# Expert tokens fetched by row numbers, and expert weights loaded in 8 KB runs, in a two-layer decoder trunk

## The chip, the core and the metric

The kernel runs on one core of a Trainium2 chip. It is written by hand, engine by engine: TensorE (PE) multiplies, VectorE (DVE) and ScalarE (ACT) read its results out of the eight PSUM banks, GpSimd (POOL) does small jobs, and SyncE (SP) issues nearly all transfers from memory. Engines wait for each other by semaphores that are written out in the code. The metric is the time of one execution on the device in microseconds.

## What is computed

A sequence of 256 tokens of width 1024, all in float32, goes through two layers. Layer 0 mixes tokens by a gated recurrence and a state-space scan, layer 1 by RWKV-7. Each layer ends in a mixture of experts, which is where most of the time and of the weights are:

```python
def grouped_moe(h, router_w, router_b, w1, w3, w2):      # 16 experts, D=1024, F=512, each token takes 2
    logits = jnp.einsum('bsd,de->bse', h, router_w) + router_b
    probs = jax.nn.softmax(logits, axis=-1)
    ...
    top_w, top_i = lax.top_k(masked, TOP_K)
    ...
    hidden = silu(einsum('bsd,edf->bsef', h, w1)) * einsum('bsd,edf->bsef', h, w3)
    hidden = hidden * gates[..., None]
    return jnp.einsum('bsef,efd->bsd', hidden, w2)
```

## The kernel before

**Experts in blocks.** The 16 experts are taken in 8 pairs. A block is 128 slots: 64 for tokens of the one expert of a pair and 64 for the other. A pair takes one block, or more where an expert has over 64 tokens; with these inputs layer 0 has 9 blocks (the fourth pair has two) and layer 1 has 8. Tables made on the chip give each pair's number of blocks, and every engine loops over the blocks of a layer.

**A block on PE** (`block_of_pair`, L1118). First the products with w1 and with w3, L1141, 16 matmuls each of 128x64 weights by 512 columns (a profile's x32 for each, since a float32 matmul stands as two records). Then `gather` (L1063, L1066): the tokens of the next block are brought into the transposed form `hgT` that the products want, by 16 matmuls of the normed tokens `hN` with a one-hot matrix `pick`. Then `scatter(0)` (L1074), which adds the previous block's result back to its tokens by another one-hot matrix `spread`; 4 transposes of the hidden layer (L1153); `scatter(1)`; and the product with w2 (L1165), first for columns 0 to 511 of the output, then for the rest.

**Around it.** DVE multiplies the two halves of the hidden layer (L2328), copies the second half of the gathered tokens (`take_b`, L2301), makes the next `pick` (`pick_step`, L2293, L2296) and the next `spread` (L2337 to L2341). ACT does the SiLU, copies the first half (`take_a`), the transposed hidden layer and half of the result. POOL has nothing to do in the blocks.

**Weights.** w1, w3 and w2 of an expert are 2 MB each. Ten slots of 2 MB hold them, that is five "doubles" (one matrix of both experts of a pair, two slots). A layer has 24 doubles. The first five are loaded before the blocks start. Double number d (from 5) goes where double d-5 was, when the last block of that pair is through with it: `w1_done`, `w3_done` and `down_half` tell SP (L626 to L631). A double goes out as four transfers of 1 MB. In each, row k*128+p of a matrix goes to partition p (`row_block`), so a transfer is made of runs of 512 numbers, 2 KB.

**Another place that is touched.** In the RWKV-7 layer, PE makes the gate (`gate_second`, four banks), which ACT reads out by `evac_T(ggT, ...)` (L1633), and then starts the next projection (`rkv(1, 0)`, L784) in the same four banks. Between them ACT takes roots of key lengths (`key_root`, L1610 and L1616), of which numbers 2 and 3 wait for DVE (L2406).

## Time and profile before

| | |
|---|---|
| median of 3 runs | 1210.8 us (1210.73 to 1210.84) |
| the profiled execution | 1203.89 us, of which the span from first to last instruction is 1202.2 us |
| granted TensorE clock over the span | 0.972 |
| moved by the transfer engines | 309.56 MB |
| L1141 and L1165, products of the experts | 1088 and 544 matmul records |
| L1066, one-hot gathers | 608 records, 72.7 us |

"Busy" in a row is the time in which an engine has an instruction in it. The chain is the work that ended last, followed back from the last instruction to whatever released it. A time in brackets behind a row is how long the engine sat idle before it, and what ended that. The granted clock is 1.00 at 2.4 GHz and 0.50 at 1.2 GHz.

### The profile page before, as it was taken

What the parts mean: (1) busy time and instruction counts of PE and PEld (TensorE: products, weight loads), DVE (VectorE), ACT (ScalarE), POOL (GpSimd) and SP (SyncE); (2) the same over time, 40 slices, a digit from 0 to 9 for tenths busy, and PEclk for the clock granted to TensorE, in tenths of its full rate; (3) what the DMA queues carried; (4) which work ended last, traced back from release to release, by engine and by line L of the source; (5) the groups of instructions that cost most, each with busy time, mean ns of one, the idle gap of its engine ahead of it and who ended that gap; (6) DMA issues with size and microseconds to landing.
All of it is one profiled execution on the core that took longest, in us unless ns stands there. A gap on an engine that the chain in (4) does not pass through costs nothing.

```text
span 1202.2 us, 15755 instructions
## 1 busy us (share of the span) xinstructions
PE 1144.8 (95%) x6555; PEld 758.4 (63%) x6555; DVE 418.5 (35%) x932; ACT 266.6 (22%) x439; POOL 90.7 (8%) x120
## 2 busy tenths in 40 slices
PE   5899999998989999999999897999989999999997
PEld 3686798984478844444444576848878744444454
DVE  0364853365720321111111485565432411111113
ACT  2222110414220311111111344233230311111112
POOL 5002221200000100000000102111000100000000
PEclk9899999999989899999999998999989899999998
DMA  9797774439967379959999712000069599999991
GB/s 351 264 340 279 280 271 149 141 129 370 402 236 262 119 291 387 386 217 349 389 386 338 286 71 70 1 0 2 7 261 387 186 335 387 387 386 386 386 382 42
DMA packets 157180, 309.56 MB, mean 258 GB/s; under 512 B 9568, under 2 KB 10940, under 8 KB 157116
## 3 DMA queue, kind: packets, MB, share of 16 engines
q1 hardware_dynamic: 156320, 307.39, 70.3%
q8 instruction: 51, 0.84, 0.3%
q10 hardware_dynamic: 796, 1.23, 0.3%
q14 instruction: 13, 0.11, 0.0%
HBM read 307.55 MB, written 1.05 MB: 257 GB/s over the span
## 4 chain that ended last, share of the span: by engine, by line
PE 90%; DVE 3%; SPq 3%; ACT 2%; DMA 1%; issue 1%; ACTq 1%; DVEq 0%
PE bank L1141 19%; PE bank L784 16%; PE bank L1165 10%; PE bank L845 7%; PE bank L1074 7%; PE bank L1066 6%; PE bank L795 5%; PE bank L911 2%; PE bank L817 1%; PE bank L754 1%; PE bank L1427 1%; SPq L509 1%; PE bank L1417 1%; PE bank L1335 1%; DMA ring<-in_ev_w_in 1%
## 5 line engine op out<-in xcount | busy, mean ns | idle before, releaser
L784 PE MATMUL bank<-arena,ring 128*128 128x256 f32 x960 | 216.2, 387 | 10.4 <-ACT arena L1633 6.3
L784 PEld LDWEIGHTS bank<-arena,ring 128*128 128x128 f32 x960 | 185.6, 195 | 37.7 <-issue 9.9
L1141 PE MATMUL bank<-ring,arena 128*64 128x512 f32 x704 | 153.7, 592 | 0.0
L1141 PEld LDWEIGHTS bank<-ring,arena 128*64 128x64 f32 x704 | 50.4, 137 | 99.6 <-issue 99.4
L2328 DVE TENSOR_TENSOR arena<-arena,bank 128x512 f32<-128x512 f32 x17 | 11.7, 687 | 220.7 <-PE bank L1141 220.7
L845 PE MATMUL bank<-arena,ring 128*128 128x256 f32 x384 | 85.4, 386 | 2.9 <-DVE arena L2551 2.9
L1074 PE MATMUL bank<-arena 128*128 128x256 f32 x336 | 84.2, 398 | 1.7 <-issue 1.7
L1141 PE MATMUL bank<-arena 128*64 128x512 f32 x384 | 84.1, 592 | 0.0
L845 PEld LDWEIGHTS bank<-arena,ring 128*128 128x128 f32 x384 | 74.4, 194 | 13.7 <-issue 3.2
L1066 PEld LDWEIGHTS bank<-arena 128*128 128x128 f32 x608 | 69.3, 192 | 13.8 <-issue 13.8
L1066 PE MATMUL bank<-arena 128*128 128x128 f32 x608 | 72.7, 278 | 0.0
L1074 PEld LDWEIGHTS bank<-arena 128*128 128x128 f32 x336 | 64.6, 202 | 11.6 <-issue 3.4
L1165 PE MATMUL bank<-ring,arena 128*64 128x512 f32 x288 | 63.8, 595 | 0.0
L1141 PEld LDWEIGHTS bank<-arena 128*64 128x64 f32 x384 | 27.6, 137 | 54.8 <-issue 54.8
L1165 PE MATMUL bank<-arena 128*64 128x512 f32 x256 | 56.7, 595 | 0.0
L795 PE MATMUL bank<-ring,arena 128*128 128x512 f32 x128 | 55.5, 592 | 0.0
L2344 DVE COPY arena<-bank 128x512 f32<-128x512 f32 x17 | 11.8, 692 | 102.3 <-PE bank L1165 102.3
L1165 PEld LDWEIGHTS bank<-ring,arena 128*64 128x64 f32 x288 | 19.9, 137 | 39.0 <-issue 39.0
L1971 DVE SCALAR_TENSOR_TENSOR arena<-ring,csilu,arena 128x512 f32<-128x512 f32 x56 | 43.6, 779 | 2.0
L1752 ACT ACTIVATE arena<-bank 128x512 f32<-128x512 f32 x19 | 11.3, 597 | 142.5 <-PE bank L1066 142.5
L795 PEld LDWEIGHTS bank<-ring,arena 128*128 128x128 f32 x128 | 24.2, 190 | 29.3 <-issue 29.2
L1762 ACT ACTIVATE arena<-bank 128x512 f32<-128x512 f32 x17 | 10.1, 597 | 139.5 <-PE bank L1141 139.5
(366 smaller groups left out, 1302.7 us busy)
## 6 DMA issues: line engine op xcount, KB each, us to landing
ring<-in_moe_w SPq DMA_DIRECT2D x112, 1024.0 KB, 14.2
arena<-in_moe_w SPq DMA_DIRECT2D x80, 1024.0 KB, 14.3
ring<-in_mod_w SPq DMA_DIRECT2D x24, 2048.0 KB, 11.1
ring<-in_ev_w_in SPq DMA_DIRECT2D x13, 2048.0 KB, 13.1
ring<-in_od_w_rkv SPq DMA_DIRECT2D x6, 2048.0 KB, 13.5
ring<-in_ev_w_out SPq DMA_DIRECT2D x4, 2048.0 KB, 17.3
ring<-in_od_w_o SPq DMA_DIRECT2D x2, 2048.0 KB, 10.5
arena<-in_x ACTq DMA_DIRECT2D x1, 1024.0 KB, 9.1
```

The source lines that it names most:

```text
L509: sp.dma_start(dst, src).then_inc(tile_landed[slot], 16)
L754: mm = pe.matmul(norm_total(k), ones[:, 0:P], squares[:, b, :], start=(b == 0), stop=(b == KB - 1))
L784: mm = pe.matmul(ps[:, c * S:(c + 1) * S], w_cols(slot)[:, k, (2 * half + c) * P:(2 * half + c + 1) * P], src[:, k, :], start=(k == 0), st ...
L795: mm = pe.matmul(ps[:, :], src[:, k, tt * P:(tt + 1) * P], w_cols(slot)[:, k, :], start=(k == 0), stop=(k == KB - 1))
L817: mm = pe.matmul(row_bank[32 * c:32 * (c + 1), :], slide[g][:, k, 31 - i:63 - i], w_cols(slot)[:, k, :], start=(m == a and r == 0), stop=( ...
L845: mm = pe.matmul(bank[d // 2][:, (d % 2) * S:(d % 2 + 1) * S], w_rows(slot)[:, kk, d * P:(d + 1) * P], srcs(4 * j + kk), start=(j == 0 and ...
L911: mm = pe.matmul(ps[:, hh * 64:(hh + 1) * 64], et, right, start=True, stop=True)
L1066: mm = pe.matmul(bank[6 + kb // 4][:, (kb % 4) * P:(kb % 4 + 1) * P], hN[:, tt, kb * P:(kb + 1) * P], pick[:, tt, :], start=(tt == 0), sto ...
L1074: mm = pe.matmul(bank[d // 2][:, (d % 2) * S:(d % 2 + 1) * S], ymoe[:, d * P:(d + 1) * P], spread, start=(first and d % 2 == 0), stop=last ...
L1141: mm = pe.matmul(bank[4 + half][e * C:(e + 1) * C, :], hgT[:, kb, e * C:(e + 1) * C], piece(slots[e], kb), start=(kb == 0), stop=(kb == KB ...
L1165: mm = pe.matmul(bank[5 + half][e * C:(e + 1) * C, :], hidT[:, f, e * C:(e + 1) * C], piece(slots[e], 4 * half + f), start=(f == 0), stop= ...
L1971: ins = stt(acc, w_cols(slot)[:, k, :], csilu[:, k:k + 1], acc, ALU.mult, ALU.add)
```

## The change

**Tokens by row number.** After the normed tokens `hN` are made, SP stores them once in each layer to a table in memory (`rows_dram`, 256 rows of 4 KB, 1 MB), whose row 256 holds zeros. For each block PE multiplies `pick` with token numbers (`slot_rows`, two matmuls of one column), DVE turns the result into whole numbers (`row_numbers`), and POOL issues an indirect transfer of 128 rows (512 KB) into `landing`, in place of `hN`. In the next block PE turns `landing` into `hgT` by 8 transposes, in place of the 16 matmuls of the one-hot gather. The gather stays for the first block of a layer. `pick` is now made one block earlier.

**Runs of 8 KB.** Partition p now gets rows 8p to 8p+7 of w1 and w3 and rows 4p to 4p+3 of w2, in two transfers each, so that a run is 8 KB. The columns of `hN` and of the hidden layer are put in the same order. w2 is taken in halves of its rows, so both halves of the output stay open until the second. A half of a double is now freed, and its load issued, when half of a product is through.

**ACT's order.** `evac_T(ggT)` goes before the roots 2 and 3. Some semaphores are merged.

```diff
+        tok_id = sb("tok_id", [P, NT])
+        slot_row = sb("slot_row", [P, 1], mybir.dt.uint32)
+        rows_dram = nc.dram_tensor("token_rows", (S + 1, D), F32, kind="Internal").ap()
+        landing = buf(2)[:, 0:D]
+        pick_next = m3[:, 8 * P:10 * P].rearrange("p (t c) -> p t c", t=NT)
...
-                    src = row_block(t[names[kind]][l, 2 * pair + e])
-                    src = src[:, :, h * W:(h + 1) * W] if kind == 2 else src[:, 4 * h:4 * h + 4, :]
-                    dst = weight_half(doubles[l][d][0][e], h).rearrange("p (k n) -> p k n", k=4)
+                    rows = 2 if kind == 2 else 4
+                    src = t[names[kind]][l, 2 * pair + e].rearrange("(p k) n -> p k n", p=P)[:, rows * h:rows * (h + 1), :]
+                    dst = weight_half(doubles[l][d][0][e], h).rearrange("p (k n) -> p k n", k=rows)
...
+                sp.wait_ge(base["hN_evac"], 4 * (l + 1))
+                sp.dma_start(rows_dram[0:S, :].rearrange("(t p) d -> p t d", p=P), hN).then_inc(stored, 16)
...
-                    if kind == 0:
-                        sp.wait_ge(base["w1_done"], done)
-                    elif kind == 1:
-                        sp.wait_ge(base["w3_done"], done)
-                    else:
-                        sp.wait_ge(base["down_half"], done * 2)
-                    double_load(d)
+                    for h in range(2):
+                        if kind == 2:
+                            sp.wait_ge(base["down_half"], done * 3 + 2 if h else done * 3)
+                        else:
+                            sp.wait_ge(base["w3_done" if kind else "w1_done"], done * 2 + 1 if h else done * 2)
+                        double_load(d, h)
...
+            def fetch_rows(l):
+                m = M[l]
+                pool.wait_ge(stored, 16 * (l + 2))
+                ...
+                def fetch():
+                    pool.indirect_dma_start(landing, None, rows_dram, bass.IndirectOffsetOnAxis(ap=slot_row[:], axis=0)
+                                            ).then_inc(m["fetched"], 16)
+                pool.wait_ge(m["spread_ready"], 2)
+                fetch()
+                with pool.Fori(1, total) as g:
+                    pool.wait_ge(m["spread_ready"], g + 2)
+                    pool.sem_inc(pool_chain, 1)
+                    fetch()
...
+                def slot_rows(ps, one):
+                    for tt in range(NT):
+                        mm = pe.matmul(ps, one[:, tt, :], tok_id[:, tt:tt + 1], start=(tt == 0), stop=(tt == NT - 1))
+                    return mm
...
                     pe.wait_ge(m["y1_ready"], g + 1)
-                    pe.wait_ge(m["pick_ready"], g + 2)
-                    gather()
-                    pe.wait_ge(m["spread_ready"], g + 1)
+                    pe.wait_ge(m["fetched"], g * 16 + 16)
+                    for kb in range(KB):
+                        mm = pe.transpose(bank[6 + kb // 4][:, (kb % 4) * P:(kb % 4 + 1) * P],
+                                          landing[:, kb * P:(kb + 1) * P], ident[:])
+                        if kb % 4 == 3:
+                            mm.then_inc(m["gath_full"], 1)
                     scatter(0)
                     pe.wait_ge(m["hid_ready"], g + 1)
                     for f in range(FB):
                         mm = pe.transpose(bank[4][:, f * P:(f + 1) * P], hid[:, f * P:(f + 1) * P], ident[:])
                     mm.then_inc(m["hidT_full"], 1)
+                    pe.wait_ge(m["hgb_ready"], g + 2)
+                    pe.wait_ge(m["pick_ready"], g + 3)
+                    slot_rows(bank[7][:, 0:1], pick)
                     scatter(1)
...
-                for u in range(4):
-                    key_root(u)
+                key_root(0)
+                key_root(1)
                 evac_T(ggT, 0)
                 evac_T(ggT, 4)
+                key_root(2)
+                key_root(3)
...
-                    tt_(hid, hsil, bank[5][:], ALU.mult).then_inc(m["hid_ready"], 1)
+                    tt_(hid.rearrange("s (f p) -> s p f", f=FB), hsil.rearrange("s (p f) -> s p f", f=FB),
+                        bank[5][:].rearrange("s (p f) -> s p f", f=FB), ALU.mult).then_inc(m["hid_ready"], 1)
...
+                    row_numbers(bank[7][:, 0:1])
                     after(stt(spread, rows4[:, 0, :], pcol[:], rows4[:, 2, :], ALU.is_equal, ALU.mult), 2)
                     tt_(spread, spread, spread2, ALU.add).then_inc(m["spread_ready"], 1)
```

PE's program in the first pair's block, before: from the w3 product to the w2 product.

```order
L1141 MATMUL bank<-ring,arena 64x512 [waits tile_landed5,tile_landed4,m0_y0_ready]
L1141 MATMUL bank<-ring,arena 64x512 x15
L1146 REGISTER_ALU [waits m0_y1_ready]
L1066 MATMUL bank<-arena 128x128 [waits m0_pick_ready]
L1066 MATMUL bank<-arena 128x128 x15
L1074 MATMUL bank<-arena 128x256 [waits m0_spread_ready]
L1074 MATMUL bank<-arena 128x256 x3
L1153 MATMUL bank<-ident,arena 128x128 [waits m0_hid_ready]
L1153 MATMUL bank<-ident,arena 128x128 x3
L1074 MATMUL bank<-arena 128x256 x4
L1165 MATMUL bank<-arena 64x512 [waits tile_landed7,tile_landed6,m0_hidT_ready]
```

The same place in the changed kernel, whose lines are numbered anew: L1178 is the product of L1141, L1186 the transposes of `landing`, L1103 the scatter, L1148 `slot_rows`.

```order
L1178 MATMUL bank<-ring,arena 64x512 [waits tile_landed5,tile_landed4,m0_spread_ready]
L1178 MATMUL bank<-ring,arena 64x512 x15
L1184 ISA [waits m0_y1_ready]
L1186 MATMUL bank<-ident,arena 128x128 [waits m0_fetched]
L1186 MATMUL bank<-ident,arena 128x128 x7
L1103 MATMUL bank<-arena 128x256 x4
L1194 MATMUL bank<-ident,arena 128x128 [waits m0_hid_ready]
L1194 MATMUL bank<-ident,arena 128x128 x3
L1197 REGISTER_ALU [waits m0_hgb_ready]
L1148 MATMUL bank<-tok_id,arena 128x1 [waits m0_pick_ready]
L1148 MATMUL bank<-tok_id,arena 128x1
L1103 MATMUL bank<-arena 128x256 x4
```

Eight transposes stand where 16 matmuls stood, behind a wait for the transfer, and two small matmuls are new ahead of the second scatter, behind waits for DVE.

ACT's program in the RWKV-7 layer, before: the roots of the key lengths and the gate's copies.

```order
L1610 ACTIVATE arena<-arena 128x512 [waits kk_max]
L1616 ACTIVATE arena<-arena 128x512 [waits stat_ln]
L1610 ACTIVATE arena<-arena 128x512 [waits kk_max]
L1616 ACTIVATE arena<-arena 128x512 [waits stat_ln]
L1610 ACTIVATE arena<-arena 128x512 [waits kk_max]
L1616 ACTIVATE arena<-arena 128x512 [waits stat_ln]
L1610 ACTIVATE arena<-arena 128x512 [waits kk_max]
L1616 ACTIVATE arena<-arena 128x512 [waits stat_ln]
L1633 ACTIVATE arena<-bank 128x512 [waits proj_full] x4
```

In the changed kernel (L1658 and L1664 are the roots, L1681 is the copy):

```order
L1658 ACTIVATE arena<-arena 128x512 [waits kk_max]
L1664 ACTIVATE arena<-arena 128x512 [waits stat_ln]
L1658 ACTIVATE arena<-arena 128x512 [waits kk_max]
L1664 ACTIVATE arena<-arena 128x512 [waits stat_ln]
L1681 ACTIVATE arena<-bank 128x512 [waits proj_full] x4
L1658 ACTIVATE arena<-arena 128x512 [waits kk_max]
L1664 ACTIVATE arena<-arena 128x512 [waits stat_ln]
```

The four copies have moved ahead of the third and fourth root.

## Rows read from the trace of the kernel before

**Rows 1.** The page: busy time of PE, transfer rate in 40 slices, the chain's shares.

```profile
PE 1144.8 (95%) x6555; PEld 758.4 (63%) x6555; DVE 418.5 (35%) x932; ACT 266.6 (22%) x439; POOL 90.7 (8%) x120
...
GB/s 351 264 340 279 280 271 149 141 129 370 402 236 262 119 291 387 386 217 349 389 386 338 286 71 70 1 0 2 7 261 387 186 335 387 387 386 386 386 382 42
...
PE 90%; DVE 3%; SPq 3%; ACT 2%; DMA 1%; issue 1%; ACTq 1%; DVEq 0%
```

**Rows 2.** The chain in order of time, blocks of experts: start us, us, what.

```profile
434.96 3.77 PE bank L1066 x32
438.73 1.73 PE bank L1074 x8
440.89 1.73 PE bank L1074 x8
442.62 7.02 PE bank L1165 x32
449.64 13.73 PE bank L1141 x64
...
956.73 13.88 PE bank L1141 x64
...
1155.78 13.73 PE bank L1141 x64
...
1177.18 7.02 PE bank L1165 x32
```

**Rows 3.** Groups of PE's instructions from 395 to 435 us: count, busy us, mean ns.

```profile
L1045 PE MATMUL bank<-router_w,modT 128*128 128x16 f32 x16 | 1.9, 257 | 0.0
L1060 PE MATMUL bank<-ident,scratch 128*128 128x1 f32 x4 | 1.0, 352 | 0.0
```

**Rows 4.** Timeline of DVE in the first block: start us, us, instruction, idle before.

```profile
435.07 0.69 DVE L2328 TENSOR_TENSOR arena<-arena,bank 128x512 f32<-128x512 f32 x1 [12.03 <-PE bank L1141]
...
438.76 0.69 DVE L2301 COPY arena<-bank 128x512 f32<-128x512 f32 x1 [3.00 <-PE bank L1066]
...
439.88 0.61 DVE L2296 SCALAR_TENSOR_TENSOR arena<-iota,tok,arena 128x128 f32<-128x128 f32 x2
```

**Rows 5.** Timeline of ACT, DVE and PE around the gate, 728 to 812 us.

```profile
743.10 0.63 ACT L1610 ACTIVATE arena<-arena 128x512 f32<-128x512 f32 x1 [3.53 <-DVE arena L2406]
...
745.47 2.04 ACT L1633 ACTIVATE arena<-bank 128x512 f32<-128x512 f32 x4
...
746.20 10.20 PE L784 MATMUL bank<-arena,ring 128*128 128x256 f32 x32 [6.25 <-ACT arena L1633]
...
758.31 7.17 PE L784 MATMUL bank<-arena,ring 128*128 128x256 f32 x32
...
742.38 1.28 DVE L2406 TENSOR_SCALAR arena<-bank 128x512 f32<-128x512 f32 x2
...
747.75 0.68 DVE L2418 TENSOR_TENSOR arena<-arena 128x512 f32<-128x512 f32 x1
```

**Rows 6.** Stretches: length, busy us of PE to POOL, granted clock, DMA share, GB/s.

```profile
749.00:752.00 3.00, 3.00 (x9) 2.37 (x8) 1.64 (x1) 0.00 (x0) 3.00 (x1) 0.50 0.00 0
```

**Rows 7.** Transfers in two stretches, 307 to 323 and 990 to 1140 us.

```profile
DMA packets 1646, 6.55 MB, mean 409 GB/s; under 512 B 48, under 2 KB 48, under 8 KB 1646
...
DMA packets 29162, 58.00 MB, mean 387 GB/s; under 512 B 884, under 2 KB 884, under 8 KB 29156
```

**Rows 8.** Timeline of SP's issues, and the stretch in which the loads end.

```profile
621.29 21.92 SPq L581 DMA_DIRECT2D arena<-in_moe_w  x8
...
963.79 12.49 SPq L581 DMA_DIRECT2D ring<-in_moe_w  x8
...
1170.00:1175.00 5.00, 5.00 (x40) 4.75 (x39) 1.96 (x6) 0.60 (x1) 0.00 (x0) 1.00 0.48 177
```

**Rows 9.** The page: transfers by issue, KB each, median us to landing.

```profile
ring<-in_moe_w SPq DMA_DIRECT2D x112, 1024.0 KB, 14.2
...
arena<-in_x ACTq DMA_DIRECT2D x1, 1024.0 KB, 9.1
```

More of the change, by code:

```diff
@@ L350, in trunk @@
                      "hidT_full", "hidT_ready", "down_half", "y0_ready", "y1_ready", "spread_ready", "scat_done",
-                     "chain"]
+                     "chain", "fetched"]
         M = [dict(shared, **{n: sem(f"m{l}_{n}") for n in moe_names}) for l in range(LAYERS)]
@@ L587, in first_load, with double_load @@
                         half_load(d, e, h, slot)
-                def double_load(d):
-                    for h in range(2):
-                        for e in range(2):
-                            half_load(d, e, h, doubles[l][d][0][h])
+                def double_load(d, h):
+                    for e in range(2):
+                        half_load(d, e, h, doubles[l][d][0][h])
                 last = [max(n for n in range(n_stage) if n % SLOTS == slot) for slot in range(SLOTS)]
@@ L1062, in moe, with gather @@
                 mm.then_inc(m["logit_full"], 1)
-                def gather():
+                def gather(first=False):
                     for kb in range(KB):
@@ L1070, in gather @@
                             mm.then_inc(m["gath_full"], 1)
+                        elif first and kb < 3:
+                            mm.then_inc(m[("w1_done", "w3_done", "down_half")[kb]], (1, 1, 2)[kb])
                 def scatter(half, first=False, last=False):
@@ L1113, in moe @@
                 pe.wait_ge(m["pick_ready"], 1)
-                gather()
+                gather(first=True)
+                pe.wait_ge(m["pick_ready"], 2)
+                def slot_rows(ps, one):
+                    for tt in range(NT):
+                        mm = pe.matmul(ps, one[:, tt, :], tok_id[:, tt:tt + 1], start=(tt == 0), stop=(tt == NT - 1))
+                    return mm
                 pe.wait_ge(m["rows_ready"], l + 1)
                 pe.wait_ge(m["tab_ready"], l + 1)
+                slot_rows(bank[5][:, 0:1], pick_next).then_inc(m["gath_full"], 1)
                 def block_of_pair(g, pair):
@@ L1724, in take_const @@
                     act.wait_ge(m["const_full"], l + 1)
[L1725 removed]
+                    act.activation(logit_const, bank[4][:, 0:NE], ACT.Copy)
                 def expert_shift(q):
@@ L2289, in moe, with pick_step @@
                 dve.wait_ge(m["slots_ready"], 2 * l + 2)
-                def pick_step(wait_for):
+                def pick_step(wait_for, pick=pick):
                     for tt in range(NT):
@@ L2309, in moe, with row_numbers @@
                 link(ts_(tok4[:, :, 0:2], tok4[:, :, 0:2], -float(P), None, ALU.add))
+                pick_step(link, pick_next).then_inc(m["pick_ready"], 1)
+                dve.wait_ge(m["pick_ready"], 2)
+                link(ts_(tok4[:, :, 0:2], tok4[:, :, 0:2], -float(P), None, ALU.add))
+                def row_numbers(ps):
+                    return ts_(slot_row[:], ps, float(S), None, ALU.add)
                 dve.wait_ge(m["rows_ready"], l + 1)
```

87 lines of the change are left out of this document (50 added, 37 removed).

## The prediction

> **What bounds the kernel now.** I read the page first [rows 1]. PE is busy 95% of the span and has 90% of the chain that ended last, so time goes where PE's time goes. But the transfer rate stands at 386 to 389 GB/s for many slices in both stretches with experts, and at 382 to 387 in six slices in a row before the last one. The reader is to see two resources close to their limits, and that PE is ahead only by a little. The chain in order of time [rows 2] then gives PE's program without a gap: a block is 28.41 us (463.37 less 434.96), of which gather 3.77, scatter 1.73, the four transposes 0.43 (440.89 less 438.73 and 1.73), scatter 1.73, w2 7.02, and w1 with w3 13.73. The first block of layer 1 starts at 956.73, the last at 1155.78, and its w2 product at 1177.18.
>
> How near are the transfers? SP issues the sixth double of layer 1 at 963.79, when w1's product of the first block is through, and the rate in the last stretch (177 GB/s in 5 us, so 2.3 us of transfer) puts the end of the loads at 1172.3 [rows 8]. Between lie 19 doubles of 4.19 MB, 79.7 MB; at the measured 387 GB/s [rows 7] these are 205.9 us, which gives 1169.7, so 2.6 us are lag. The transfers of layer 1 thus run without a pause, and end 4.9 us before PE wants the last of them. That slack is all there is: what PE gains in layer 1 it keeps only if the transfers get shorter too. In layer 0 SP's last issue ends at 643.2 [rows 8], landing near 653, and the last w2 product starts at 669.9 (442.62 plus 8 blocks), so 17 us are free.
>
> **Part 1, ACT's order.** PE sat idle 6.25 us at 746.20 for the gate's copies, and the projection behind it, 32 records, took 10.20 us where the same 32 take 7.17 later [rows 5]: the granted clock was 0.50, the 1.2 GHz level, behind that idle time [rows 6]. ACT ended the second root at 739.56 and then waited 3.53 us for DVE, with the copies queued behind [rows 5]. In the new order the first copy (0.6 us) ends near 740.2 and PE starts then: 6.0 us earlier. With no idle time worth the name the clock should stay, which gives back 3.0 more. The four copies end at 741.6, before DVE's lengths (743.66), so roots 3 and 4 are not later. What is late next: the key products of PE need DVE's keys, the last at 748.4 [rows 5], and PE comes for these near 756. Gain 9.0 us; at least 6.0 if the clock drops all the same.
>
> **Part 2, the gather.** Removed: 3.77 us a block. Added on PE: 8 transposes. The four of the hidden layer take 0.43 [rows 2], so 0.86. Then `slot_rows`, two float32 matmuls of one column, four records. The nearest rows are L1060, four such records in 1.0 us, and L1045, 16 of 16 columns in 1.9, so 0.12 each [rows 3]. Here they stand in a full stream, as L1045's do, so I take 0.46, and 1.0 as the bound. A block gets shorter by 3.77 - 0.86 - 0.46 = 2.45 us; at worst, with transposes as costly as half the gather's matmuls (1.9) and slot_rows at 1.0, by 0.9.
>
> Does the new wait for DVE bite? Count from the end of w3. DVE multiplies from 0.1 to 0.8; its store is now strided, and were it twice as slow it would end at 1.5. `take_b` can start when the transposes are through, 1.0, and from its start to the end of `pick_step` are 1.73 us (438.76 to 440.49 [rows 4]). So `pick` is ready near 2.8, or 3.3. PE comes for it at 0.86 + 1.73 + 0.43 = 3.0. It is hidden, by 0.2 us only; 0.3 us a block, 5 us in all, if the strided store is slow. DVE's `row_numbers` delays `spread` by some 0.2 us, and the next user of that is 19 us away.
>
> The fetch is triggered after scatter(1) and about 1.1 us of DVE, 6.5 us after the end of w3, and wanted at the next end of w3, 26.0 us after this one. It has 19.5 us for 0.5 MB, which at 387 to 409 GB/s are 1.3 us of the engines. In a layer's first block it has about 13, with the transfer engines nearly idle ahead of it. The store of 1 MB in each layer falls into the same idle time, needs 2.6 us at 409 GB/s, and only DVE's first multiplication waits for it, 14 us later. I cost both at nothing on PE. POOL, otherwise idle in the blocks, does them; behind them it has the scaling of the RWKV-7 ranks, whose weights come later than the last fetch.
>
> Once a layer `slot_rows` is added ahead of the first block, 0.46. Layer 0 is held by PE: 9 x 2.45 - 0.46 = 21.6 us. Its transfers have 17 us of slack against the 21.6 by which PE comes earlier. But they pause while the fourth pair takes its second block (217 GB/s in that slice [rows 1]), and the pause now ends 12.7 us earlier: four blocks of 2.45, half a w1 product of 3.4, less 0.5. Five fetches in the stretch behind it cost 6.5 of that. So 23 us are free against 21.6 even at the old rate.
>
> **Part 3, layer 1 and the 8 KB runs.** PE alone would gain 8 x 2.45 - 0.46 = 19.1 us. The transfers: packets of 4 KB ran at 409 GB/s, of 2 KB at 387 [rows 7]. Per engine of 16 that is 160 and 85 ns, so 2 KB more cost 75 and each packet 10; 8 KB would take 310 ns, 422 GB/s. Bounds: 387 if length does nothing, 409 if runs are split at 4 KB, 437 above (75 ns for every 2 KB and nothing for the packet). I take 420, by the slope between the two rows.
>
> The tight place is the second half of w3 in the last block. Its weights are the end of double 22: 18 doubles and 7 fetches, 75.5 + 3.7 = 79.2 MB, from 960.8 (963.8 plus the 0.5 of slot_rows, less half of w1, 3.4), with a lag of 2.6. At 420 GB/s: 188.5 us, 1151.9. PE comes at 957.2 + 7 x 25.96 + 10.3 = 1149.2. It waits 2.7 us, and layer 1 gains 16.4. At 409 it waits 7.7 and gains 11.4. At 387 it waits 18.7 and gains 0.4: then the fetches would have eaten what the early release gave.
>
> The Trainium skill (DMA: Bandwidth & Descriptors, "Why small descriptors are slow") gives the cost of a packet as about 3 cycles of the bus inside the engine, at 32 bytes a cycle. By it 8 KB would run 1.2% faster than 4 KB, 414 GB/s, PE would wait 5.4 us and layer 1 gain 13.7, so the whole would be 1166. Its step from 2 to 4 KB is 2.3%, and the rows show 5.7%, so I go by the rows.
>
> **Sum.** 9.0 + 21.6 + 16.4 = 47.0 us. Against the profiled execution (1203.89, span 1202.2) that is 1156.9; its runs without a profile have a median 6.9 us above it, and I carry that along: 1210.8 - 47.0 = 1163.8, say 1164.
>
> **Rivals.**
> *The transfers hold layer 1 harder.* 8 KB runs bring 0 to 5.7% and not 8.5%, or indirect rows cost more than their bytes. For it: the 4.9 us of slack. Against: 4 KB packets are faster, and that is measured. Layer 1 gains 11.4 to 0.4, with a clock that may drop in the waits: 1169 to 1180. Chance 0.22.
> *The fetch is late, and the kernel slower.* Every block would wait for `fetched`. If L is the time from trigger to landing, 17 blocks lose L - 19.5 each; from 47/17 = 2.8 us on, that is L = 22.3, the kernel is slower than before. At L = 24 it is 1240 (17 x 4.5 = 76 lost of which 47 are covered). For it: loads of SP take 14.2 us to land, being queued behind 5.5 MB [rows 9], and fewer, longer packets could let that queue hold more bytes; no row shows an indirect transfer. Against: a transfer on another queue does not wait for SP's. The 1 MB of x, on ACT's queue, landed in 9.1 us while SP had four loads of 2 MB out [rows 9], some 21 us of transfers. Chance 0.13.
> The Trainium skill (same page, "Queues, rings and completion order") says that each engine takes turns between the queues it has work for, packet by packet. By that the fetch's 8 packets of an engine would wait for about as many of SP's, some 4 us, and the time would stay 1164.
> *The change saves less on PE* (a wait for DVE, dearer transposes, blocks 1.5 shorter): layer 0 gains 13, layer 1 up to 11.5, part 1 gives 6 to 9, so 1177 to 1180. Chance 0.07.
>
> **How the numbers follow.** The forecast, 1158 to 1169, has 0.55; the second rival's 1169 to 1180 has 0.22 and the last 0.07; late fetch 0.13, split into slower (0.11) and a mild lateness below that; the rest 0.03. Range 1158 to 1180. Below 1158 there is only the case without any wait at the end and a cheaper slot_rows (1161 less 3). A measurement of this kernel can tell about 0.2% from no change. Faster by more than that: 0.86; within it 0.03; slower 0.11.
>
> **What would show it.** Part 1: PE idle under 0.5 us ahead of the projection and 7.1 us for its first 32 records. Part 2: in the chain of layer 0, blocks of 26.0 us, with 8 transposes of 0.86, and no wait for POOL or DMA of `landing`. Part 3: a rate near 420 GB/s, and PE waits of 2 to 3 us on `in_moe_w` only in the last block of layer 1. I would be wrong if PE waits in every block, if the rate stays at 387, or if a wait drops the clock in the blocks.

## The result, and the profile after

The changed kernel takes 1165.46 us (median of four runs, 1160.99 to 1168.27), the kernel before, run beside it, 1210.82. The ratio is 0.962, with a 95% interval from 0.9583 to 0.9657. The profiled execution took 1162.93 us with a span of 1161.2, against 1203.89 and 1202.2. So 45.4 us are gone by the medians and 41.0 by the two profiles; the prediction had 47.0 and 1164.

These lines of the page after answer to [rows 1] and [rows 9] (the last two are issues: KB each, median us from issue to landing):

```profile
PE 1105.4 (95%) x6223; PEld 719.1 (62%) x6223; DVE 428.9 (37%) x951; ACT 266.7 (23%) x439; POOL 107.4 (9%) x138
...
GB/s 350 267 371 290 263 172 279 84 145 259 390 293 342 164 197 422 421 421 287 421 420 420 344 104 21 53 0 3 2 199 420 210 401 420 421 420 420 421 421 85
DMA packets 86452, 320.55 MB, mean 276 GB/s; under 512 B 9877, under 2 KB 11253, under 8 KB 61813
...
PE 83%; SPq 6%; DMA 4%; DVE 3%; ACT 2%; issue 1%; ACTq 1%; DVEq 0%
...
ring<-in_moe_w SPq DMA_DIRECT2D x112, 1024.0 KB, 16.0
arena<-in_moe_w SPq DMA_DIRECT2D x80, 1024.0 KB, 19.0
```

PE has 39.4 us less work and the same share of the span. The rate in the full slices of the experts is 420 to 422 GB/s, where [rows 1] has 386 to 389. Of the chain SPq and DMA together now hold 10%, which was 4%: near the end the chain runs through the weights of layer 1.

The chain in order of time (start us, us, what), to be set against [rows 2]:

```profile
424.66 0.34 PE bank L1148 x4
425.00 13.88 PE bank L1178 x64
438.88 1.03 PE bank L1186 x8
...
451.27 13.73 PE bank L1178 x64
465.00 1.02 PE bank L1186 x8
466.03 1.73 PE bank L1103 x8
467.76 0.44 PE bank L1194 x4
468.19 0.34 PE bank L1148 x4
468.53 1.83 PE bank L1103 x8
470.37 7.02 PE bank L1211 x32
477.39 3.00 PE bank L1178 x13
...
661.47 3.72 PE bank L1103 x16
...
1098.73 28.26 DMA arena<-in_moe_w
1126.99 0.04 issue
1127.03 3.65 PE bank L1178 x16
```

L1178 is w1 and w3, L1186 the transposes of the fetched rows, L1103 a scatter, L1194 the hidden layer's transposes, L1148 `slot_rows`, L1211 w2. A block is 26.12 us (477.39 less 451.27) where it was 28.41. The last rows are the second half of w3 in the last block of layer 1, which waits for a load issued 28.3 us earlier. The waits of PE on weights (us in all, times, longest), then the stretch 957 to 1120 us (length, busy us of PE to POOL, granted clock, DMA share, GB/s), and two stretches around that wait:

```profile
PE bank L1178 <- DMA arena<-in_moe_w: 2.1, 2, 1.2
```

```profile
957.00:1120.00 163.00, 163.00 (x800) 70.73 (x798) 31.26 (x79) 22.93 (x31) 5.63 (x6) 1.00 1.01 420
...
1125.00:1127.00 2.00, 0.80 (x4) 0.00 (x0) 0.00 (x0) 0.00 (x0) 0.00 (x0) 1.00 1.02 426
1130.00:1140.00 10.00, 10.00 (x56) 6.07 (x54) 4.40 (x12) 1.19 (x2) 0.00 (x0) 1.00 0.55 229
```

PE is never idle for 163 us while the transfers run at 420 GB/s. Then it waits 2.1 us, 0.9 ahead of the first half of w3 and 1.2 ahead of the second, with the clock at 1.00.

What the fetch and the strided store do in a block, by the timelines of DVE and POOL (start us, us, instruction, idle before):

```profile
465.05 1.07 DVE L2386 TENSOR_TENSOR arena<-arena,bank 128x512 f32<-128x512 f32 x1 [13.04 <-PE bank L1178]
466.06 0.69 DVE L2353 COPY arena<-bank 128x512 f32<-128x512 f32 x1
466.67 0.48 DVE L2345 TENSOR_SCALAR arena<-iota,tok 128x128 f32<-128x128 f32 x2
467.18 0.61 DVE L2348 SCALAR_TENSOR_TENSOR arena<-iota,tok,arena 128x128 f32<-128x128 f32 x2
```

```profile
472.20 0.94 POOL L730 DMA_INDIRECT arena<-token_rows,slot_row  x1 [25.14 <-DVE arena L2400]
```

The store with a stride takes 1.07 us and not 0.69 [rows 4]; `pick` is ready at 467.79, 2.8 us after the end of w3, and PE comes for it at 468.19. The fetch is issued 7.2 us after the end of w3. Its time from issue to landing over all 17, and the wait of PE at the gate, which answers to [rows 5]:

```profile
DMA to landing us min/median/max: 4.4/8.6/10.0
```

```profile
722.50 7.15 PE L811 MATMUL bank<-arena,ring 128*128 128x256 f32 x32 [0.25 <-ACT arena L1681]
...
721.78 2.04 ACT L1681 ACTIVATE arena<-bank 128x512 f32<-128x512 f32 x4
```

**Where the time came from**, by matching points of the chains of before and after:

| point | before | after | shift |
|---|---|---|---|
| first block of layer 0 starts | 421.07 | 425.00 | +3.9 |
| its last scatter starts | 677.79 | 661.47 | -16.3 |
| the section with the gate starts | 705.17 | 687.48 | -17.7 |
| it ends | 767.47 | 740.72 | -26.7 |
| first block of layer 1 starts | 956.73 | 931.41 | -25.3 |
| its last scatter starts | 1185.04 | 1144.05 | -41.0 |

Layer 0's experts give 20.2, the gate 9.1, layer 1's 15.7. The 3.9 us lost ahead of all that are the subject of the first experiment. Ahead of the gate 1.4 us came beside these: 32 records took 5.07 us before, with the granted clock at 0.79 from 686 to 694 us, and the same 32 took 3.67 after, at 1.00. Ahead of layer 1's experts 1.4 went again, of which 0.34 are `slot_rows`.

### The profile page after: what moved, and what is told of

The parts are those of the page before. It is cut to its first block, busy times and chain, and to the rows that moved or that the text cites. A ratio compares the mean times of both kernels' runs of the same rounds, so it can differ in the third digit from the quotient of the medians.

```text
span 1161.2 us, 15296 instructions
## 1 busy us (share of the span) xinstructions
PE 1105.4 (95%) x6223; PEld 719.1 (62%) x6223; DVE 428.9 (37%) x951; ACT 266.7 (23%) x439; POOL 107.4 (9%) x138
## 2 busy tenths in 40 slices
DMA packets 86452, 320.55 MB, mean 276 GB/s; under 512 B 9877, under 2 KB 11253, under 8 KB 61813
## 3 DMA queue, kind: packets, MB, share of 16 engines
q0 software_dynamic: 2448, 8.91, 2.0%
## 4 chain that ended last, share of the span: by engine, by line
PE 83%; SPq 6%; DMA 4%; DVE 3%; ACT 2%; issue 1%; ACTq 1%; DVEq 0%
PE bank L1178 17%; PE bank L811 17%; PE bank L1211 9%; PE bank L872 7%; PE bank L1103 6%; PE bank L822 5%; SPq L585 3%; PE bank L938 2%; DMA arena<-in_moe_w 2%; PE bank L844 1%; PE bank L1186 1%; PE bank L781 1%; PE bank L1475 1%; SPq L513 1%; PE bank L1465 1%
## 5 line engine op out<-in xcount | busy, mean ns | idle before, releaser
L1178 PE MATMUL bank<-ring,arena 128*64 128x512 f32 x704 | 153.7, 592 | 0.0
L1178 PEld LDWEIGHTS bank<-ring,arena 128*64 128x64 f32 x704 | 50.4, 137 | 99.4 <-issue 99.4
L2386 DVE TENSOR_TENSOR arena<-arena,bank 128x512 f32<-128x512 f32 x17 | 18.1, 1068 | 224.5 <-PE bank L1178 224.5
L1178 PE MATMUL bank<-arena 128*64 128x512 f32 x384 | 84.4, 593 | 2.1 <-DMA arena<-in_moe_w 2.1
L1103 PE MATMUL bank<-arena 128*128 128x256 f32 x336 | 84.3, 398 | 2.0 <-DVE arena L2404 2.0
L1103 PEld LDWEIGHTS bank<-arena 128*128 128x128 f32 x336 | 63.6, 199 | 11.5 <-issue 3.7
L1211 PE MATMUL bank<-ring,arena 128*64 128x512 f32 x288 | 63.8, 595 | 0.0
L1178 PEld LDWEIGHTS bank<-arena 128*64 128x64 f32 x384 | 27.6, 137 | 57.4 <-issue 55.3
L1211 PE MATMUL bank<-arena 128*64 128x512 f32 x256 | 56.7, 595 | 0.0
L730 POOL DMA_INDIRECT arena<-token_rows,slot_row x17 | 16.2, 956 | 394.5 <-DVE arena L2400 315.7
L1211 PEld LDWEIGHTS bank<-ring,arena 128*64 128x64 f32 x288 | 19.9, 137 | 39.0 <-issue 39.0
L2064 DVE SCALAR_TENSOR_TENSOR arena<-bank,modT,arena 128x256 f32<-128x256 f32 x32 | 13.6, 479 | 74.5 <-PE bank L872 69.8
L1681 ACT ACTIVATE arena<-bank 128x512 f32<-128x512 f32 x28 | 16.2, 599 | 104.0 <-PE bank L822 54.4
L1802 ACT ACTIVATE arena<-bank 128x512 f32<-128x512 f32 x19 | 11.3, 597 | 121.4 <-PE bank L1186 119.0
## 6 DMA issues: line engine op xcount, KB each, us to landing
ring<-in_ev_w_in SPq DMA_DIRECT2D x13, 2048.0 KB, 12.8
ring<-in_od_w_rkv SPq DMA_DIRECT2D x6, 2048.0 KB, 13.3
ring<-in_od_w_o SPq DMA_DIRECT2D x2, 2048.0 KB, 10.2
```

The lines of the kernel that those rows point to most:

```text
L730: pool.indirect_dma_start(landing, None, rows_dram, bass.IndirectOffsetOnAxis(ap=slot_row[:], axis=0)).then_inc(m["fetched"], 16)
L1103: mm = pe.matmul(bank[d // 2][:, (d % 2) * S:(d % 2 + 1) * S], ymoe[:, d * P:(d + 1) * P], spread, start=(first and d % 2 == 0), stop=last ...
L1178: mm = pe.matmul(bank[4 + half][e * C:(e + 1) * C, :], hgT[:, kb, e * C:(e + 1) * C], piece(slots[e], kb), start=(kb == 0), stop=(kb == KB ...
L1211: mm = pe.matmul(bank[5 + half][e * C:(e + 1) * C, :], hidT[:, f, e * C:(e + 1) * C], weight_half(slots[e], rows)[:, v:v + W], start=(f == ...
L1681: act.activation(dst, bank[n % 4][:], func, **kw).then_inc(proj_evac, 1)
L2386: tt_(hid.rearrange("s (f p) -> s p f", f=FB), hsil.rearrange("s (p f) -> s p f", f=FB), bank[5][:].rearrange("s (p f) -> s p f", f=FB), A ...
```

## The experiments

Each time is a median on the chip; the kernel before ran beside each group: 1210.84, 1212.92 and 1209.93 us in the three groups, with single runs from 1203.9 to 1215.3. "Stage" is the time from a layer's first block to its last scatter, in the profile. It leaves out what the clock does elsewhere, and in the three profiles of the changed kernel it repeats within 0.3 us in layer 0 and within 1.0 in layer 1.

| kernel | median (range) | ratio to before (95%) | stage of layer 0 | of layer 1 |
|---|---|---|---|---|
| before | see above | 1 | 256.7 | 228.3 |
| changed, first time | 1165.46 (1161.0 to 1168.3) | 0.962 (0.9583 to 0.9657) | 236.5 | 212.6 |
| changed, once more | 1165.26 (1161.4 to 1169.3) | 0.9635 (0.9599 to 0.967) | 236.2 | 213.6 |
| ACT's order alone | 1199.92 (1198.4 to 1202.5) | 0.9916 (0.989 to 0.9943) | 256.7 | 228.3 |
| 8 KB runs alone | 1209.44 (1201.5 to 1214.8) | 0.9995 (0.9967 to 1.0023) | 256.7 | 228.3 |
| without the fetch | 1161.91 (1157.8 to 1167.2) | 0.9585 (0.9548 to 0.9622) | 236.2 | 210.1 |
| fetch twice | 1171.5 (1170.1 to 1176.2) | 0.9683 (0.9645 to 0.9722) | 236.2 | 223.5 |
| old runs of 2 KB | 1178.26 (1174.5 to 1182.7) | 0.975 (0.9702 to 0.9798) | 236.2 | 226.8 |
| late release | 1169.69 (1161.4 to 1171.7) | 0.9655 (0.9593 to 0.9716) | 236.2 | 216.5 |
| empty places skipped | 1160.46 (1158.3 to 1164.5) | 0.9602 (0.9555 to 0.9649) | 236.2 | 210.1 |
| changed, third time | 1167.13 (1164.6 to 1168.9) | 0.9656 (0.9627 to 0.9685) | 236.4 | 213.3 |
| empty places skipped, again | 1160.13 (1159.0 to 1161.7) | 0.9601 (0.9575 to 0.9627) | 236.2 | 210.1 |
| fetch after w2 | 1164.03 (1159.3 to 1169.6) | 0.9651 (0.9611 to 0.9691) | 236.2 | 214.8 |
| fetch after w1 | 1214.24 (1205.1 to 1217.0) | 1.0036 (1.0014 to 1.0058) | 263.3 | 232.8 |

**The changed kernel once more.** No edit.

> The changed kernel once more. It has a spread of 7 us over four runs, where the kernel before has 1. Theory: the clock. In the first profile a wait of 2.1 us near 117 us was followed by a stretch at 0.50 that cost 4.6 us and that the kernel before did not have behind the same wait; runs near 1161 lack it. Then the first block of layer 0 starts near 420.4 or near 425.0 in this profile, and the two layers of experts take 236.5 and 212.6 us again, within 0.5. Rival: the transfers. Then the start is the same and the layer 1 stage differs by 3 to 7 us, with PE waits for in_moe_w of that size.

The runs of the kernel before spread over 9 to 11 us in the three groups, those of the changed kernel over 4 to 8, so the spread is not of the change. One source of it the timelines of PE show, first of the changed kernel's first profile, then of this one, with a stretch of it by windows:

```profile
117.49 7.06 PE L938 MATMUL bank<-arena 128*128 128x64 f32 x32 [2.09 <-DVE arena L2115]
```

```profile
117.75 3.76 PE L938 MATMUL bank<-arena 128*128 128x64 f32 x32 [2.09 <-DVE arena L2115]
...
172.50 4.65 PE L938 MATMUL bank<-arena 128*128 128x64 f32 x32
176.94 16.53 PE L811 MATMUL bank<-arena,ring 128*128 128x256 f32 x64
```

```profile
176.00:180.00 4.00, 4.00 (x13) 3.41 (x13) 2.81 (x2) 0.00 (x0) 2.69 (x2) 0.50 1.05 389
```

The same 32 instructions behind the same wait of 2.09 us took 7.06 us in one execution (granted clock 0.50 from 118 to 122) and 3.76 in the other; there the clock fell to 0.50 at 176, with PE busy all the while. The kernel before had the wait too, and 3.76 us behind it in its profile. The +3.9 us ahead of layer 0's experts are thus 0.34 of `slot_rows` and, for the rest, a clock that fell in this execution at a place that the change doesn't touch. (Over all profiles that first block starts anywhere from 420.9 to 430.4 us with the new gather and from 421.1 to 426.5 with the old one.) It fits this that the profiled execution of before lay 6.9 us below its median and that of the changed kernel 2.5: the profiles give 41.0 us and the medians 45.4.

**ACT's order alone**, in the kernel before:

```diff
-                for u in range(4):
-                    key_root(u)
+                key_root(0)
+                key_root(1)
 ...
+                key_root(2)
+                key_root(3)
```

> The kernel before with the two roots behind the gate's copies, nothing else. Theory: 6.0 us of idle time and 3.0 us of a half clock go, so 1201.8, and the 32 records of L784 behind the gate take 7.1 us. Rival 1: the clock drops all the same, 1204.8. Rival 2: the wait moves on to the key products, 1208 to 1211.

```profile
744.24 7.14 PE L784 MATMUL bank<-arena,ring 128*128 128x256 f32 x32 [0.25 <-ACT arena L1633]
```

10.9 us less by the medians (9.0 were expected, and the two agree within the spread of the runs), and in the profile the section with the gate takes 53.24 us (709.22 to 762.46) where it took 62.30: 9.06, exactly what it takes in the changed kernel. The idle time of 6.25 us is 0.25, and the 10.20 us behind it are 7.14. Part 1 stands by itself and adds up.

**8 KB runs alone.** The kernel before, with the new order of rows on partitions, w2 by halves of its rows and the release by halves, but with the gather by products (the lines of the loads; the rest follows from them):

```diff
-                    src = row_block(t[names[kind]][l, 2 * pair + e])
-                    src = src[:, :, h * W:(h + 1) * W] if kind == 2 else src[:, 4 * h:4 * h + 4, :]
+                    rows = 2 if kind == 2 else 4
+                    src = t[names[kind]][l, 2 * pair + e].rearrange("(p k) n -> p k n", p=P)[:, rows * h:rows * (h + 1), :]
```

> The kernel before with the 8 KB runs, the orders that belong to them and the early release, but with the one-hot gather and the old order of ACT. Theory: PE holds it, transfers only get more slack: blocks of 28.4 us, 1210.8 within 1 us, with a rate of 421 GB/s. Rival (shorter transfers are worth something by themselves): some us faster.

No change that can be told, and both stages to 0.1 us what they were. The transfers did get faster: from 1000 to 1150 us they run at 420 to 422 GB/s, and are through soon after 1150 where the loads of the kernel before end near 1172 by the prediction's reckoning (this run's layer 1 starts 2.4 us earlier). That is worth nothing while PE's block is 28.4 us.

**Old runs of 2 KB, with the new gather.** The changed kernel, with this undone (and with it the strided copies that belong to it):

```diff
-                    src = t[names[kind]][l, 2 * pair + e].rearrange("(p k) n -> p k n", p=P)[:, rows * h:rows * (h + 1), :]
+                    src = row_block(t[names[kind]][l, 2 * pair + e])[:, rows * h:rows * (h + 1), :]
```

> The changed kernel with runs of 2 KB for w1 and w3 and of 4 KB for w2 (row k*128+p on partition p, as before), and the tokens' and hidden columns in their plain order. Theory: layer 1 is held by bytes over rate. Twelve doubles at 387, six and the fetches at 409 GB/s are 200.5 us up to the last half of w3, against 188 at 421, so PE waits 13 to 14 us in all where it waits 2.1, the stage goes from 212.6 to 224.5 and the whole to about 1177. Rival (the length of runs does nothing for the end): 1165. Layer 0 stays at 236.5.

PE's waits, the stretch 957 to 1120 and the fetches' landing:

```profile
PE bank L1177 <- DMA ring<-in_moe_w: 8.6, 5, 2.8
...
PE bank L1177 <- DMA arena<-in_moe_w: 5.1, 3, 2.9
```

```profile
957.00:1120.00 163.00, 154.37 (x754) 67.45 (x752) 27.92 (x77) 20.15 (x28) 5.63 (x6) 1.00 1.04 395
```

```profile
DMA to landing us min/median/max: 5.3/7.0/7.6
```

The waits are 13.7 us, as expected; the stage is 226.8 and not the 224.5 expected, for two reasons that *Fetch twice* below shows as well: the granted clock was 0.86 from 1120 to 1130 us, and each wait costs some 0.2 us beyond its length. Layer 1's stage gains only 1.5 us on the kernel before, against 15.7 with 8 KB. So the same 8 KB that were worth nothing without the gather's change are worth some 14 us with it: 13.3 to 14.2 in the stage, 12.8 by the medians of different groups.

**Without the fetch.** POOL signals and moves nothing, so all blocks but a layer's first multiply what happens to stand in `landing`, and the output is wrong.

```diff
-                    pool.indirect_dma_start(landing, None, rows_dram, bass.IndirectOffsetOnAxis(ap=slot_row[:], axis=0)
-                                            ).then_inc(m["fetched"], 16)
+                    pool.sem_inc(m["fetched"], 16)
```

> The changed kernel without the indirect transfers: POOL raises the semaphore at once, so all blocks but a layer's first multiply stale tokens. Theory: the fetch costs PE nothing but its 3.7 MB in layer 1 (8.7 us of the engines), of which 2.1 us show as PE's waits in the last block; the layer 1 stage goes from 212.6 to 210.4 and layer 0 stays at 236.5, in all 2.3 us less. Rival (the fetch delays each block a little, or disturbs DVE or PE): layer 0 gets shorter too, by 0.1 to 0.5 us a block, and the whole by 4 to 10.

Layer 0's stage is what it was, to 0.3 us, and blocks are 26.11 us. Layer 1's is 210.05, 2.6 to 3.5 less, with no wait for weights. So a fetch costs PE nothing by its latency, and what it costs is bandwidth, in layer 1 only.

**Fetch twice.** A second fetch of the same rows goes beside the first, and PE waits for both.

```diff
+                    pool.indirect_dma_start(buf(2)[:, D:2 * D], None, rows_dram, bass.IndirectOffsetOnAxis(ap=slot_row[:], axis=0)
+                                            ).then_inc(m["fetched"], 16)
...
-                    pe.wait_ge(m["fetched"], g * 16 + 16)
+                    pe.wait_ge(m["fetched"], g * 32 + 32)
```

> The changed kernel with two indirect transfers for each block, the second into memory that nothing reads. Theory: layer 0 stays at 236.5 (its transfers have room); layer 1 is held by the transfers, and 3.7 MB more at 421 GB/s are 8.7 us, so its stage goes from 212.6 to 221.3 and the whole by 8.7 up. Rival (the fetch has room of its own): nothing changes. Rival (the fetch is near its limit of 19.5 us from trigger to landing): waits in every block, 20 us or more.

PE's waits for weights are 10.2 us, near what was expected and 7.4 to 8.1 more than in the changed kernel. Layer 1's stage is 223.5, 9.9 to 10.9 more. The seven or eight fetches that fall into the stretch in which the transfers never pause are 8.7 to 10.0 us at 420 GB/s. So once the transfers bind, bytes go over to PE about one for one. What the stage has beyond the waits is shown by PE's timeline:

```profile
1093.50 5.35 PE L1180 MATMUL bank<-arena 128*64 128x512 f32 x16 [2.64 <-DMA arena<-in_moe_w]
...
1125.86 3.65 PE L1180 MATMUL bank<-ring,arena 128*64 128x512 f32 x16 [2.63 <-DMA ring<-in_moe_w]
```

Behind the first wait the granted clock was 0.76 from 1093 to 1100 us, and 16 records took 1.7 us longer than behind a second wait of the same length. And 16 records that stand behind a wait take 3.65 us, where in the stream they take 3.43 (13.73/4). With six waits, 210.05 + 10.2 + 1.7 + 6 x 0.22 are 223.3.

**Late release.** SP waits for a whole product before it loads either half.

```diff
-                            sp.wait_ge(base["down_half"], done * 3 + 2 if h else done * 3)
+                            sp.wait_ge(base["down_half"], done * 3 + 2)
...
-                            sp.wait_ge(base["w3_done" if kind else "w1_done"], done * 2 + 1 if h else done * 2)
+                            sp.wait_ge(base["w3_done" if kind else "w1_done"], done * 2 + 1)
```

> The changed kernel in which a double's both halves wait until its product is through. Theory: the transfers of layer 1 start 3.4 us later and never catch up, so PE waits 5.5 us in place of 2.1 and the whole gets 3.4 us longer; layer 0 stays. Rival: nothing, if the end is held by something else.

The waits for weights are 5.5 us (2.9 on the ring's, 2.6 on the arena's) against 2.1, and the stage is 216.5, 3.0 to 3.9 us longer than in the changed kernel. The release by halves is worth what half a w1 product takes, 3.4 us.

**Empty places skipped.** A block has 128 places, and many are empty; those pointed at the row of zeros, and fetched it. With a bound the transfer doesn't move their rows, and what stands in `landing` from before is multiplied by weights of zero at the scatter.

```diff
-                    pool.indirect_dma_start(landing, None, rows_dram, bass.IndirectOffsetOnAxis(ap=slot_row[:], axis=0)
-                                            ).then_inc(m["fetched"], 16)
+                    pool.indirect_dma_start(landing, None, rows_dram, bass.IndirectOffsetOnAxis(ap=slot_row[:], axis=0),
+                                            bounds_check=S - 1, oob_is_err=False).then_inc(m["fetched"], 16)
```

> The changed kernel in which rows for empty slots are skipped (an index over 255 moves nothing). About half of the slots are empty, so the seven fetches of layer 1 move 1.8 MB less, 4.4 us of the engines. Theory: PE's waits of 2.1 us in the last block go, the stage from 212.6 to 210.4, the whole 2.3 us down. Rival: no change, or a fetch that takes longer to issue.

The queue of the fetches moves 3.48 MB in place of 8.91. Its packets are 2,448 as before: the program's packets under 512 B are 1,329 more (11,206 for 9,877), and in the last fetch of each layer, which is for a block that doesn't exist, all have 4 bytes. So an empty place still costs a packet, and the median landing is 8.0 us where it was 8.6. Layer 1's stage is 210.05, the same as without any fetch, and no wait for weights is left. The first medians alone (1160.46 and 1165.46, of different groups) didn't tell the two kernels apart, so both ran again side by side.

> The changed kernel once more, on the same chip and in the same rounds as the next three, so that differences of 2 to 3 us between them can be told. Theory: a median near 1165, runs from 1161 to 1169; the first block of layer 1 to its last scatter 212.6 to 213.6 us, with waits of PE for in_moe_w of 2.1 to 2.6 us in the last block of layer 1 alone.

> The fetch skips the rows of empty places once more, now in the same rounds as the changed kernel. Theory (the transfers of layer 1 are 2 to 3 us short of hiding behind PE, and the skipped rows are what is over): the stage of layer 1 takes 210.05 us, 2.6 to 3.5 less than in the changed kernel, and the median is lower by as much. Rival (the difference of the earlier runs was that of the clock ahead of layer 0's experts, which lies elsewhere in each execution): the medians agree within 1 us.

1160.13 against 1167.13, and no run of the one within the range of the other (1159.0 to 1161.7, 1164.6 to 1168.9). The stages differ by 3.2 us (213.26 less 210.06); the other 3.8 us of the medians lie elsewhere, and the two profiles show what can put them there: the first block of layer 0 starts at 424.75 in the one and at 429.85 in the other, where the granted clock is 0.55 from 122 to 130 us. I count 3 us as shown, and the rest as the spread of the runs. It is the fastest kernel of the study by its medians.

**The fetch made late.** Two doses, to test the rival that the prediction gave 0.13. POOL also waits for w2 of the block ahead, or for w1 of the block whose end needs the rows:

```diff
                     pool.wait_ge(m["spread_ready"], g + 2)
+                    pool.wait_ge(m["down_half"], g * 3 + 2)
```

```diff
                     pool.wait_ge(m["spread_ready"], g + 2)
+                    pool.wait_ge(m["w1_done"], g * 2 + 3)
```

> From a layer's second fetch on POOL also waits for the end of the w2 product ahead, so that each of 15 fetches starts about 5.3 us later (477.5 in place of 472.2 in the first blocks) and has 13.6 us to the end of w3. Theory: a fetch needs what it needed in the changed kernel, at most 10.0 us from its issue to its landing, so no block waits and the time stays near 1165. Rival (a fetch that starts later meets a fuller queue of SP's loads and lands later still): waits of PE ahead of the transposes, and over 1170.

> From a layer's second fetch on POOL also waits for the end of the w1 product of the block whose end needs the rows, so that each of 15 fetches has 6.9 us. Theory: with landings of 4.4 to 10.0 us, 8.6 in the middle, a block waits 1.8 us (27 us in all), of which the 2.6 us of layer 1's wait for weights come back; if TensorE's clock stays, the time is near 1190; if it falls to 0.50 behind each wait, as it did once behind 2.1 us, another 1 to 2 us a block, 1205 to 1215. Rival (what made the landings long was where in the block the fetches started, and here they land in under 6.9 us): no change, 1165.

With 12.9 us to go to the end of w3 (13.6 were expected) nothing is lost: 1164.03, no wait for a fetch, and landings of 4.0, 9.4 and 10.0 us (least, middle, most). Only layer 1's stage is 1.2 to 2.2 us longer, with 4.1 us of waits for weights; why is open. With some 6 us to go the whole gain is gone and more, 1214.24. In that kernel (the transposes' waits; the timeline of POOL and of PE; a stretch by windows; the landings):

```profile
PE bank L1187 <- DMA arena<-token_rows,slot_row: 33.8, 13, 3.4
```

```profile
486.21 0.94 POOL L730 DMA_INDIRECT arena<-token_rows,slot_row  x1 [30.03 <-PE bank L1179]
...
485.24 7.04 PE L1179 MATMUL bank<-arena 128*64 128x512 f32 x32
495.65 1.47 PE L1187 MATMUL bank<-ident,arena 128*128 128x128 f32 x8 [3.37 <-DMA arena<-token_rows,slot_row]
496.91 3.24 PE L1104 MATMUL bank<-arena 128*128 128x256 f32 x8
```

```profile
495.00:498.00 3.00, 2.35 (x11) 2.18 (x12) 0.85 (x3) 0.60 (x1) 0.00 (x0) 0.70 1.03 429
```

```profile
DMA to landing us min/median/max: 3.9/8.6/9.4
```

PE waits 2.6 us a time, 33.8 in all, and runs slower behind most of the waits: here the eight records of scatter(0) take 3.24 us and not 1.89, and the granted clock from 495 to 498 is 0.70. So it is behind nine of the 13 waits, where transposes and scatter(0) together take 1.4 to 1.7 us longer, 14.8 in all; behind the other four, of 1.05, 2.48, 2.65 and 2.71 us, they take their usual time. My expectation was short by 24 us (1190) where the clock stays and near the upper one (1205 to 1215) where it falls: the clock falls, most times. The stages lost 27.1 and 19.5 us, 46.6 together, of which the waits are 33.8; the difference of 12.8, and the 2 to 3 us of waits for weights that this kernel no longer has, are that work at a lower clock. The landing depends little on where the fetch starts: 8.6, 9.4 and 8.6 us in the middle for the three starts.

## Why the prediction was right, point by point

**What bounds the kernel** was read rightly: PE by a little, and the transfers of layer 1 with under 5 us of slack. The two experiments on the runs show it from both sides: 8 KB without the new gather gain nothing, the new gather with 2 KB gains 1.5 us in layer 1. The prediction had 0.4 us for the second.

**Part 1, ACT's order**: 9.0 predicted, 9.05 in the changed kernel and 9.06 alone. Both halves came, 6.0 of idle time and 3.0 of clock.

**Part 2, the gather**: the block's terms, predicted and measured:

| term | predicted | measured |
|---|---|---|
| 8 transposes | 0.86 | 1.02 |
| `slot_rows` | 0.46 | 0.34, and 0.10 more in the scatter behind it |
| block | 25.96 | 26.12 |
| `pick` ready after the end of w3 | 2.8 | 2.8 |
| layer 0 | 21.6 | 20.2 in the stage, less 0.34 ahead of it |

The mis-sized term is the transposes, by 0.16 us: I took 0.107 us each from the four of the hidden layer. By the starts in the trace they follow each other every 0.109 us in both places, the eight of the first block at 438.82, 438.98, 439.09 and so on; the 0.16 lies between the end of w3's product and the end of the first of them (0.27 us, not 0.109). The old gather had such a step too: 32 records take 3.77 us behind w3 and 3.57 ahead of a layer's first block. So the change of product is paid before and after, and I had counted it only in what was removed. Nine blocks of 0.16 are 1.4 of the 1.7 us that layer 0 falls short. In the layer's last block the chain has 0.61 us for `slot_rows` and not 0.34: DVE's two steps for `pick` took 0.63 and 0.82 us there, not 0.48 and 0.61, beside POOL's scaling of ranks (from 645.71), and the first weights for `slot_rows` waited 0.27 us for DVE. That is the rest. The store with a stride did become slow, 1.07 us and not 0.69, but less than the doubled time I had allowed for, and stayed hidden by 0.4 us; that it would cost 0.3 a block didn't come true.

**The fetch** had 19.5 us by the prediction and 18.9 by the timeline (472.20 to the end of w3 at 491.1), and needs 8.6, at most 10.0. The rival of the late fetch fell, and the two doses show by how much: with 6 us less to go nothing is lost, and with 13 us less 47 us are. The rival's own reckoning, 2.8 us a block or 47 us of waits for the kernel to be slower than before, was too high: with 33.8 us of waits it is slower already (1.0036, interval 1.0014 to 1.0058), because the clock adds some 15 us, which the rival had left out.

Why 8.6 us, for 1.3 us of transfer? The trace shows it. Queue by queue (q1 is SP's, q0 the fetches'; packets, MB, share of 16 engines), for the fetch issued at 472.20, first from 472.2 to 476.3 us, then to 480.2:

```profile
q1 hardware_dynamic: 228, 1.70, 99.7%
...
q1 hardware_dynamic: 161, 1.14, 70.2%
q0 software_dynamic: 144, 0.52, 33.7%
```

For 4.1 us nothing of the fetch moves. Then its 144 packets, on each engine eight of 4 KB and one of 4 bytes, run for 3.9 us among SP's, about one for one: 134 of SP's 8 KB packets start between the fetch's first and its last. It has landed 0.6 us later. Eight packets of each kind on an engine are 8 x (0.31 + 0.16) = 3.8 us, with 0.31 for 8 KB on one of 16 engines at 421 GB/s. With SP's packets at 2 KB the fetch's packets run for 2.1 us, where 8 x (0.085 + 0.16) are 2.0, and the median landing is 7.0. The Trainium skill (DMA: Bandwidth & Descriptors, "Queues, rings and completion order") says that each engine takes turns between its queues, a packet at a time. The trace agrees, with one record of the profile for a packet, 134 against 128; a typical packet of the page holds 9 to 17 descriptors, while here the end of a fetch's record falls together with the start of one of SP's, not of its own next one, so a turn is one record. The prediction's "some 4 us" was this part alone.

The other part is 4.1 us from the issue to the first packet. It is 1.6 us for the fetch issued at 526.27 in the kernel *fetch after w2*, beside which SP's queue moved next to nothing, and that one landed in 4.0 us. So 4.0 us are the fetch's own, and 4.6 come from the loads beside it: 2.5 ahead of its first packet, which no run explains, and the rest by the turns and at the end. It does not wait for all that was issued before it: in the changed kernel's stretch from 990 to 1110 us SP's loads land in 27.7 us in the middle, and the fetches in 9.8.

**Part 3, layer 1**: a rate of 420 was taken and 420 to 421 measured, so the slope between the rows for 2 and 4 KB holds at 8. By the Trainium skill (DMA: Bandwidth & Descriptors, "Why small descriptors are slow"), with some 3 cycles for each packet, it was to be 414 GB/s; the measurement, 1.5% higher, decides against it. The wait, 2.7 us predicted, is 2.1 in the first profile and 2.6 in the two others, in the last block: 0.9 of the 2.1 at the first half of w3, where the prediction had the second half alone. PE starts the second half 195.6 us after the first block's start, by the prediction 194.7 (1151.9 less 957.2). The stage gained 15.7, from which `slot_rows` ahead of it takes 0.34: 15.3 against 16.4, and 14.4 and 14.7 in the two other profiles. *The transfers hold layer 1 harder* fell with the rate. What that rival feared, that indirect rows cost more than their bytes, fell with the fetch made twice: 7.4 to 8.1 us of waits, and 9.9 to 10.9 in the stage, for 8.7 to 10.0 of bytes.

**The sum**: 9.05 + 19.9 + 15.3 are 44.3 by the stages, 45.4 by the medians, 47.0 predicted. The shortfall of 2.7 by the stages is 1.7 in layer 0 and 1.1 in layer 1. It is smaller than the spread between single runs, so that the median came within 1.5 us of the forecast shows less than the stages do; in part that is luck.

## What to carry to other kernels

Find the second resource and its slack before an edit to the first is priced: here 8% of transfer rate were worth nothing before PE's block got shorter, and 13 us after. A DMA on a queue of its own may be issued late as long as its landing time, measured under the real load, fits with a margin; past that point each wait costs its length and what the clock loses behind it. And if an indirect fetch has places that hold nothing, bound its index so that they move no bytes.

## What the runs showed that I had not expected

- The granted clock fell to 0.50 with PE fully busy (176 to 180 us in one execution), and behind one and the same wait of 2.09 us it fell in one execution and stayed in another. Runs of one kernel spread by 3 to 13 us. The profiles show the clock as one source; of the runs without a profile only the mean granted clock is on record, for example 0.972 at 1169.3 us and 0.976 at 1164.2. Stages of 210 to 257 us repeated within 1.
- Waits of 1 us in the last block (2.1 in two pieces) left the clock at 1.00. Behind waits of 2.4 to 3.4 us it fell nine times of 12 in one kernel, and two waits of 2.63 and 2.64 us in another kernel differed in it as well.
- An indirect fetch of 128 rows of 4 KB occupies POOL for 0.94 us. With a bound it takes 0.99, and moves 39% of the bytes here, in as many packets.
- Beside a full queue of loads a fetch's first packet started 4.1 us after its issue, beside an empty one 1.6.
- Behind w3's product the first float32 transpose ended after 0.27 us and each further one after 0.109; four behind a scatter took 0.44 in all.
